# Four parts of a tile's head products between the levels of the next tile, with a second buffer for the masked matrices

## What is computed

```python
def gla_scan(q, k, v, loga, s0):
...
    def step(S, inp):
        qc, kc, vc, ac = inp
        b = jnp.cumsum(ac, axis=2)
        diff = b[:, :, :, None, :] - b[:, :, None, :, :]
        decay = jnp.exp(jnp.where(mask, diff, -jnp.inf))
        attn = jnp.einsum('bhid,bhjd,bhijd->bhij', qc, kc, decay)
        o = attn @ vc + jnp.einsum('bhid,bhde->bhie', qc * jnp.exp(b), S)
...
def even_mix(h, s_f, s_b, w_in, w_gate, b_gate, g_gla, w_out):
...
    o = o_f + flip(o_b)
    o = o * lax.rsqrt(jnp.mean(o * o, axis=-1, keepdims=True) + EPS)
    o = o.transpose(0, 2, 1, 3).reshape(B_, L, GLA_VAL_WIDTH) * g_gla.astype(jnp.float32)
    o = (o * jax.nn.silu(r.astype(jnp.float32))).astype(h.dtype)
    y = jnp.concatenate([fourier_mix(u_f), o], axis=-1) @ w_out
```

## Time and profile before

| | |
|---|---|
| median of 3 runs | 4030.51 us (4028.72 to 4032.40) |
| profiled execution | 4025.92 us |
| its span | 4024.1 us |
| TensorE matmuls, VectorE, ScalarE, POOL busy | 96%, 55%, 21%, 15% of the span |
| the stage of levels and heads | 2472 to 2617 us of the span |

### The profile page before, as it was taken

One profiled execution on the slowest core, in us unless ns is written; L12 is line 12 of the kernel. 1 busy time (PEld: TensorE's weight loads), 2 busy tenths in 40 slices (PEclk: granted clock), 3 DMA queues, 4 the chain that ended last, 5 costly groups with the idle time before them and its releaser, 6 DMA issues.

```text
span 4024.1 us, 46147 instructions
## 1 busy us (share of the span) xinstructions
PE 3866.8 (96%) x17618; PEld 2307.7 (57%) x17618; DVE 2207.2 (55%) x3634; ACT 837.5 (21%) x1639; POOL 599.3 (15%) x944
## 2 busy tenths in 40 slices
PE   8999999999999999999999998899999999999998
PEld 5677455544455555458744645645555444758863
DVE  0354533366566556544556015737787765438876
ACT  1266111100122322211101114521100012531000
POOL 1000000133222431400132002200000430000023
PEclk9999999999999999999999998999999999999999
DMA  5355021355412222312344212411112452002234
GB/s 190 108 192 185 21 63 53 115 170 175 156 48 91 87 75 74 126 45 92 126 168 146 73 42 85 168 44 53 63 53 73 168 182 68 16 22 84 94 126 162
DMA packets 209784, 410.59 MB, mean 102 GB/s; under 512 B 5939, under 2 KB 92297, under 8 KB 209441
## 3 DMA queue, kind: packets, MB, share of 16 engines
q1 hardware_dynamic: 203712, 386.94, 28.4%
q0 software_dynamic: 5856, 20.73, 1.7%
HBM read 405.49 MB, written 2.16 MB: 101 GB/s over the span
## 4 chain that ended last, share of the span: by engine, by line
PE 88%; DVE 6%; ACT 3%; DMA 1%; issue 1%; POOL 1%; DVEq 0%; ACTq 0%; POOLq 0%; SPq 0%
PE PS L1210 28%; PE PS L1305 19%; PE PS L1170 5%; PE PS L1143 3%; PE PS L1784 3%; PE PS L1121 3%; PE PS L1798 3%; PE PS L913 2%; PE PS L1785 1%; PE PS L1945 1%; PE PS L1955 1%; PE PS L1429 1%; PE PS L1398 1%; PE PS L1123 1%; PE PS L1632 1%
## 5 line engine op out<-in xcount | busy, mean ns | idle before, releaser
L1210 PE MATMUL PS<-UT,RING 128*128 128x384 f32 (+1 forms) x2432 | 693.8, 433 | 10.8 <-ACT BIG L3011 9.7
L1210 PEld LDWEIGHTS PS<-UT,RING 128*128 128x128 f32 x2432 | 461.0, 190 | 205.5 <-issue 15.5
L1210 PE MATMUL PS<-BIG,RING 128*128 128x384 f32 (+1 forms) x1824 | 528.4, 433 | 0.8 <-DVE BIG L2846 0.5
L1210 PEld LDWEIGHTS PS<-BIG,RING 128*128 128x128 f32 x1824 | 346.0, 190 | 147.1 <-DVEq L2020 1.1
L1305 PE MATMUL PS<-RING,BIG 128*128 128x512 f32 x810 | 377.2, 593 | 2.8 <-POOL RES_TMP L3611 1.4
L3606 POOL TENSOR_TENSOR RES_TMP<-BIG 128x128 f32<-128x128 f32 x68 | 35.7, 525 | 1677.5 <-DVE BIG L2852 581.3
L2695 DVE TENSOR_TENSOR RING<-RING 128x512 f32<-128x512 f32 x135 | 107.0, 793 | 273.6 <-DMA RING<-ff_w_dram 161.5
L1305 PEld LDWEIGHTS PS<-RING,BIG 128*128 128x128 f32 x810 | 151.2, 190 | 183.2 <-issue 177.4
L1305 PE MATMUL PS<-RING,GATE 128*128 128x512 f32 x536 | 244.0, 596 | 6.1 <-DVE RING L2698 6.1
L1305 PE MATMUL PS<-RING,RES_TMP 128*128 128x512 f32 x544 | 245.3, 593 | 0.6 <-DVE RING L2698 0.6
L1305 PEld LDWEIGHTS PS<-RING,GATE 128*128 128x128 f32 x536 | 102.1, 191 | 136.6 <-issue 125.3
(11 more groups left out here) (467 smaller groups left out, 5821.1 us busy)
## 6 DMA issues: line engine op xcount, KB each, us to landing
RING<-ff_w_dram SPq DMA_DIRECT2D x112, 1024.0 KB, 5.0
RING<-w_mod_dram SPq DMA_DIRECT2D x48, 2048.0 KB, 8.0
RING<-w_ffn_down_dram SPq DMA_DIRECT2D x55, 1024.0 KB, 5.0
RING<-w_ffn_up_dram SPq DMA_DIRECT2D x44, 1024.0 KB, 5.1
RING<-ssm_w_in_dram SPq DMA_DIRECT2D x8, 2048.0 KB, 7.8
RING<-ssm_w_out_dram SPq DMA_DIRECT2D x4, 2048.0 KB, 8.2
RING<-w_even_in_dram SPq DMA_DIRECT2D x4, 2048.0 KB, 8.3
GATE<-gates_dram POOLq DMA_DIRECT2D x12, 512.0 KB, 9.3
```

Source lines behind the costliest of these rows:

```text
L1210: m = mm(bank(bank_, n), a[:, k, :], b[:, k, :], start=k == 0, stop=k == 3)
```

## The change

A second masked matrix is laid into the place of the latent feed-forward gates, `GATE[:, 1, 0, :]`; even tiles use GB, odd tiles GATE. The four head products of tile t-1 become calls `head(t - 1, h)` behind levels 0, 1, 2 and 3 of direction 0 of tile t; those of the last tile stay at the end. ScalarE's squares and root of tile t-1 move from the end of step n = 2t-1 to step n = 2t, behind the copy of `mod_columns` and ahead of the decays. VectorE clears the second buffer in step 0 behind level 4, and waits, from tile 2 on, for the heads of tile t-2. The feed-forward gates of this layer are loaded after the first residual.

```diff
-        C_AT = GB[:, 1, :].rearrange("p (d h i) -> p d h i", d=2, h=4)
+        C_AT = tuple(x.rearrange("p (d h i) -> p d h i", d=2, h=4) for x in (GB[:, 1, :], GATE[:, 1, 0, :]))
...
+                def head(t, h):
+                    if h == 0:
+                        if t == 0:
+                            pe.wait_ge(S("L2_states_ready"), 1)
+                        pe.wait_ge(S("L2_attention_ready"), 2 * t + 2)
+                        go_bank[t] = 4 + place(go)
+                    b = go_bank[t]
+                    rows, a = slice((h % 2) * 64, (h % 2) * 64 + 64), h // 2
+                    ops = [(C_AT[t % 2][:, dr, h % 2 * 2 + a, :], C_V[:, t, h * 128:(h + 1) * 128]) for dr in range(2)]
+                    ops += [(C_QB[rows, 2 * dr + a, t * 128:(t + 1) * 128], C_S[rows, dr * 6 + t, a * 128:(a + 1) * 128])
+                            for dr in range(2) if t != first[dr]]
+                    for j, (x, y) in enumerate(ops):
+                        m = mm(bank(b + h % 2, 128, a * 128), x, y, start=j == 0, stop=j == len(ops) - 1)
+                    if h == GLA_H - 1:
+                        m.then_inc(go.full, 1)
...
                             if v_ == 1 and 2 in next_of and t + dr:
                                 mod_columns(3, 2 * t + dr - 1, 7, MOD_ROWS[2])
+                            if t and dr == 0 and 1 <= i <= GLA_H:
+                                head(t - 1, i - 1)
...
                     if t:
                         turn(t - 1)
...
+                for h in range(GLA_H):
+                    head(NT - 1, h)
...
-                    if t:
-                        dve.wait_ge(go.full, t)
+                    if t >= 2:
+                        dve.wait_ge(go.full, t - 1)
...
+                        if n == 0 and v_ == 4:
+                            step(V.memset(GATE[:, 1, 0, :], 0.0))
...
-                    if (L, q, tile, h) == (0, 0, 0, 0):
-                        dve.wait_ge(S("gates_in"), gates_so_far(0))
+                    if L in (0, 2) and (q, tile, h) == (0, 0, 0):
+                        dve.wait_ge(S("gates_in"), gates_so_far(L))
...
-                dve.wait_ge(S("gates_in"), gates_so_far(L) if L else 32)
+                dve.wait_ge(S("gates_in"), gates_so_far(L) - (32 if L in (0, 2) else 0))
...
                     if n and 2 in next_of:
                         mod_columns(3, n - 1, 7)
+                    if dr == 0 and t:
+                        head_roots(t - 1)
...
-                    if dr == 1:
-                        act.wait_ge(go.full, t + 1)
-                        for h in range(GLA_H):
-                            step(A(C_JUNK, bank(4 + h % 2, 128, h // 2 * 128), ACT.Square, accum_out=ST2[:, 32 + h:33 + h]))
-                        step(A(ST2[:, 36:40], ST2[:, 32:36], ACT.Sqrt, scale=1.0 / GLA_DV, bias=EPSC))
-                        post("head_rms_ready")
+                head_roots(NT - 1)
...
-                    spread_gates(L)
+                    spread_gates(L, (0,))
...
+                    if L == 2:
+                        spread_gates(L, (1,))
```

More of the change, by code:

```diff
@@ L1567, in turn @@
                     m.then_inc(gt.full, 1)
+                first = [o[0] for o in gla_orders()]
+                go_bank = {}
+                def head(t, h):
[13 more added lines that the diff above has]
+                        m.then_inc(go.full, 1)
                 for t in range(NT):
                     for dr in range(2):
-                        for v_ in LEVEL_ORDER:
+                        for i, v_ in enumerate(LEVEL_ORDER):
                             if v_ in (0, 4):
@@ L2393, in mixer2 @@
                         data = PS[:, i % 2 * 1024:i % 2 * 1024 + 1024].rearrange("p (s x) -> p s x", s=2)[:, :, 0:256]
-                        at = C_AT[:, dr].rearrange("p (s a) i -> p s (a i)", s=2)
+                        at = C_AT[t % 2][:, dr].rearrange("p (s a) i -> p s (a i)", s=2)
                         if v_ == 7:
@@ L3287, in turned, with head_roots @@
                     give(gt, A(C_MIX[:, 4:8, t * 128:(t + 1) * 128], bank(6).rearrange("p (a b) -> p a b", a=4), ACT.Copy))
+                def head_roots(t):
+                    act.wait_ge(go.full, t + 1)
+                    for h in range(GLA_H):
+                        step(A(C_JUNK, bank(4 + h % 2, 128, h // 2 * 128), ACT.Square, accum_out=ST2[:, 32 + h:33 + h]))
+                    step(A(ST2[:, 36:40], ST2[:, 32:36], ACT.Sqrt, scale=1.0 / GLA_DV, bias=EPSC))
+                    post("head_rms_ready")
                 for n in range(2):
```

## The result

The changed kernel takes 4038.93 us, the median of 20 runs (4031.44 to 4049.25), where the kernel before took 4031.41 in 20 runs beside them (4025.80 to 4037.41). The ratio is 1.0022, with a 95% interval of 1.0015 to 1.0029: 6 to 12 us slower. The forecast was 4031.2 with no difference; the measured median lies above the range. A second measurement in a later session gave 4040.06 in 11 runs against 4031.74, ratio 1.0021 (1.0012 to 1.0030).

The account below looks back on a forecast made before the run. TensorE was taken as busy 96% of the span, with ScalarE's decays setting the tile period; 0.9 - 0.2 + 0.6 + 0.6 - 0.7 - 0.5 = +0.7 us, put on the 4030.51 median, gave 4031.2, range 4027.0 to 4037.0.

Parts of the forecast that it names:

- the two microseconds: VectorE's level 7 copy starts at C + 3.87 instead of C + 5.86; level 4 was to give this gain back.
- C: Time reference per tile: the end of the level 6 copy with which tile t-1 ends on VectorE.
- ScalarE's root becomes the late one: First direction: root ends at C + 13.65, decays start at C + 13.7; the differences would have allowed C + 13.15.
- The period of 26.0: Time per tile with the change: decays at C + 13.7 plus 12.3 to the next C; 25.37 us before.
- The whole sum: All terms of the change together: +0.7 us, or up to +2.0 if tile 4's cold stretch is missing.
- the saved hand-over: TensorE, 64-row head group to 64-row level: 0.2 us saved at each of three places; line 922 left out.
- The memset: Clearing 128 x 1024 on VectorE in tile 0: 0.91 us plus 0.02 to issue, +0.9 on the path.
- The first rival: The 13.1 us VectorE wait ahead of level 7 goes in full: at best 4018.3 us; chance 0.05.
- the second rival: TensorE clock halves from level 1 to level 4, 5.4 us per tile: 4036.6 or 4042.0; chance 0.09 one tile, 0.06 more.
- the 0.6 us more at line 922: TensorE's idle in the second direction, lengthened by 0.6 us in each of tiles 2 and 3.
- The forecast of tile 4: -0.7 us: its late burst, 3.35 us of idle before, now falls in the time of the differences.
- The rival of the drain: A 1.28 us pause beside ScalarE's table load in tiles 1 to 4: +5.1, 4036.3 us; chance 0.03.

Follow-up runs that it names:

- experiment 2: The changed kernel plus useless TensorE products in both idle places, 7 ahead of level 1 and 8 ahead of line 922; 4030.89 us, ratio 0.9999.
- experiment 3: The kernel before the change plus 6 useless TensorE products ahead of line 922 in the second direction; 4028.58 us, ratio 0.9996.
- experiment 5: The changed kernel plus only the 7 useless TensorE products ahead of level 1 of the first direction; 4036.39 us, ratio 1.0013.
- experiment 10: The changed kernel with head parts 0 and 1 behind level 0, part 2 behind level 1, part 3 behind level 2; 4034.50 us, ratio 1.0008.

## Why the prediction was wrong

**Right: the work at full clock.** The burst leaves the place between tiles, level 7 follows the differences, the chain of levels and parts gives the two microseconds back (level 4 at C + 10.86, forecast 10.91), and ScalarE's root becomes the late one (decays at C + 13.77, forecast 13.7). The period of 26.0 stood in tiles 2 to 4 of experiment 2. The whole sum held too: with tile 4 counted like 2 and 3 it was +2.0, and the stages of experiments 2 and 3 differ by 2.5. From the copy of level 2 to that of level 3 and on to level 4 it took 1.74 and 1.64 us where the saved hand-over gave 1.72. That level 4 fits so closely is in part luck, for two misses cancel: level 7 was copied 0.2 late (C + 4.08, behind 0.22 us of idle after the differences), and at line 922 the 0.2 was saved too, which the sum had left out (1.79 us from the copy of level 1 to that of level 2, forecast 1.98). The memset was 0.91, with 0.17 of issue where 0.02 was put. The first rival, that the wait goes in full, was rightly set low: the wait went, and came back ahead of other levels.

**Wrong: the chance of the clock.** The step that failed is the second rival's "against it": that the fall had come in the second direction, and that "by the time of level 7 the head burst ran 0.64 apart again". That holds for a kernel in which the burst is there. The change takes this burst away and puts an idle of TensorE in its place, ahead of level 1, of 0.4 to 2.8 us (1.7 or more in three of five tiles). It could be had from my own numbers: level 1 starts at C + 4.65, and the work ahead of it, level 7, level 0 and head part 0, is four groups 0.64 apart, an estimated 2.6 us behind the turn (in tile 3 it ended at C + 3.1). I used this time as slack, since it hides head part 0, and did not list it as a new idle, while I counted only the 0.6 us more at line 922. The runs showed the clock falling behind it, and no fall in the chain when it was filled (experiments 2 and 5). The price of the rival was about right: 5.4 us for a cold tile, measured 4.4 in the first direction (15.5 where a warm one is 11.1). For two cold tiles it gives 4026.6 + 10.8 = 4037.4 against the profiled execution's own time, which with two cold tiles was 4037.33; that it fits so closely is in part chance, since a second direction was slow as well and other terms moved. Its chance, 0.15 in all, was far too small: all 31 timed runs of the change had a mean clock of 0.989 or less, as 23 of 95 of the kernel before had.

**A consequence missed.** The forecast of tile 4, -0.7 for a delay that would now be hidden, became +3.9. The delay was hidden (level 7 was copied at C + 4.08), but tile 4's chain was cold (15.4 us for 11.1).

The rival of the drain did not come. The Trainium skill, ScalarE: Activation LUTs, What ACT_TABLE_LOAD costs, gives a drain of about 1380 ns beside the load for every switch of sets. In the changed kernel too the root starts 0.01 us behind its load (2529.01 + 1.28, 2530.30), so the trace does not agree. The Trainium skill, TensorE: Matmul & The Clock Gate, Part 1, says that the throttled clock is the default and that activity releases it. The trace agrees: behind the idle of 1.76 us the granted clock was 0.50, and 1.00 again from 2560 on, with TensorE busy all the time between. This sentence, read against an idle that the change adds, would have been the one to weigh.

## What to carry to other kernels

List every idle of TensorE that a reordering creates, in slack as well, and ask what stands right behind it: with a serial chain of small products there, a clock that falls to half cost more here than the wait that was removed. Work that keeps TensorE busy in a pause can have a worth of its own; ask what a burst bridges before you move it. And look for the cheap edit beside the planned one: moving four squares and a root on ScalarE out of the way of the decays gained 5 to 6 us with a ratio of 0.9985, which the spreading was meant to and did not.

## What the runs showed of the hardware that was not expected

TensorE's granted clock fell to 1.2 GHz behind pauses of 1.3 us (experiment 10) to 2.8 us (the change), in a stage in which the engine was busy for 124.57 of 148 us, and behind the short ones not every time: in the kernel before, the pause at line 922 was 1.28 us in tiles 1 to 4, and the clock of the second direction was 0.89 and 0.80 in tiles 1 and 3, 1.00 in 2 and 4. Useless products in the pauses (rows of 1.8 and 2.1 us, 15 products in a tile) brought the kernel from 4038.93 us (ratio 1.0022) to 4030.89 (0.9999). Filling only the pause at line 922 did not help (4046.62, ratio 1.0040): the one ahead of level 1 then was 2.5 us in tiles 2 to 4, where it had been 0.40, 1.76 and 1.72.
